# The rows of the second and later experts' tokens by an indirect transfer from DRAM instead of a one-hot matmul

## The reference

```python
def moe_swiglu(h, router_w, wg, wu, wd):
    logits = (h @ router_w).astype(jnp.float32)
    top_val, top_idx = lax.top_k(logits, TOP_K)
    w = jax.nn.softmax(top_val, axis=-1)
    gate = jnp.sum(jax.nn.one_hot(top_idx, N_EXPERTS, dtype=jnp.float32) * w[..., None], axis=-2).astype(h.dtype)
    out = jnp.zeros_like(h)
    for e in range(N_EXPERTS):
        out = out + gate[..., e:e + 1] * swiglu(h, wg[e], wu[e], wd[e])
    return out
```

## Time and profile before

| what | value |
|---|---|
| median of 3 runs | 1684.62 us |
| profiled execution: its own time | 1684.51 us |
| its span, first to last instruction | 1682.8 us |
| busy: PE, DVE, ACT, POOL | 1589.7, 1250.4, 1077.1, 23.4 us |
| mean granted TensorE clock | 0.961 of full speed |
| DRAM read and written | 432.49 MB, 1.05 MB |

### The profile page before, as it was taken

The page is one execution under the profiler, slowest core; times in us unless marked ns, Lnnn a source line. Parts: engine busy times, 40 slices in busy tenths (PEclk is TensorE's granted clock), DMA queues, the critical chain, the costliest instruction groups (busy, mean ns, idle before and its releaser), DMA issues.

```text
span 1682.8 us, 21706 instructions
## 1 busy us (share of the span) xinstructions
PE 1589.7 (94%) x7714; PEld 1317.2 (78%) x7715; DVE 1250.4 (74%) x1354; ACT 1077.1 (64%) x1276; POOL 23.4 (1%) x52
## 2 busy tenths in 40 slices
PE   6988789998999976999999999999999999999997
PEld 5767678886888766788888888888888888888885
DVE  4545345555524743898998998998998998998996
ACT  4454344444425451787877877877877877877874
POOL 5000000000000000000000000000000000000000
PEclk9999799999968996999999999999999999999999
DMA  9510244666421142799999999999999999999960
GB/s 359 202 46 0 76 150 158 217 226 237 166 101 51 35 141 100 255 388 357 357 359 344 370 360 346 363 364 339 376 359 337 376 353 343 371 361 342 365 247 25
DMA packets 199808, 434.15 MB, mean 258 GB/s; under 512 B 6906, under 2 KB 35668, under 8 KB 199764
## 3 DMA queue, kind: packets, MB, share of 16 engines
q1 hardware_dynamic: 197184, 432.22, 71.1%
q0 software_dynamic: 288, 1.05, 0.2%
q10 hardware_dynamic: 2292, 0.28, 0.1%
HBM read 432.49 MB, written 1.05 MB: 258 GB/s over the span
## 4 chain that ended last, share of the span: by engine, by line
PE 91%; DVE 4%; ACT 3%; issue 1%; ACTq 1%; DVEq 0%
PE ps L1145 18%; PE ps L1150 18%; PE ps L1147 18%; PE ps L637 8%; PE ps L640 7%; PE ps L643 7%; PE ps L768 3%; PE ps L1116 2%; PE ps L1171 1%; PE ps L709 1%; PE ps L733 1%; DVE f_w_lo L1631 1%; PE ps L951 1%; ACT f_w_hi L1249 1%; DVE hT_lo L1643 1%
## 5 line engine op out<-in xcount | busy, mean ns | idle before, releaser
L2140 DVE TENSOR_TENSOR w_lo<-ring,w_hi 128x1024 fp32r<-128x1024 f32 x672 | 813.5, 1224 | 55.7 <-ACT w_hi L1556 15.7
L1556 ACT ACTIVATE w_hi<-ring 128x1024 fp32r<-128x1024 f32 x672 | 712.3, 1062 | 185.0 <-PE ps L1150 185.0
L1145 PE MATMUL ps<-w_hi,x_hi 128*128 128x512 f32 x896 | 354.0, 395 | 2.4 <-DVE x_lo L2146 2.4
L1147 PE MATMUL ps<-w_hi,x_lo 128*128 128x512 f32 x896 | 350.0, 391 | 0.0
L1631 DVE TENSOR_TENSOR f_w_lo<-ring,f_w_hi 128x1024 fp32r<-128x1024 f32 (+1 forms) x139 | 169.0, 1225 | 145.3 <-ACT f_w_hi L1249 144.9
L1150 PE MATMUL ps<-w_lo,x_hi 128*128 128x512 f32 x896 | 276.6, 390 | 0.0
L1249 ACT ACTIVATE f_w_hi<-ring 128x1024 fp32r<-128x1024 f32 (+1 forms) x139 | 145.1, 1056 | 163.6 <-PE ps L643 155.1
L637 PE MATMUL ps<-f_w_hi,hT_hi 128*128 128x512 f32 (+2 forms) x480 | 187.2, 394 | 19.9 <-DVE hT_lo L1643 10.3
L1145 PEld LDWEIGHTS ps<-w_hi,x_hi 128*128 128x128 f32 x896 | 168.7, 188 | 36.8 <-issue 2.6
L1150 PEld LDWEIGHTS ps<-w_lo,x_hi 128*128 128x128 f32 x896 | 168.5, 188 | 36.3
L1147 PEld LDWEIGHTS ps<-w_hi,x_lo 128*128 128x128 f32 x896 | 168.8, 188 | 34.1
(11 more groups left out here) (250 smaller groups left out, 1284.9 us busy)
## 6 DMA issues: line engine op xcount, KB each, us to landing
ring<-in_moe_w_gate SPq DMA_DIRECT2D x56, 2048.0 KB, 8.5
ring<-in_moe_w_up SPq DMA_DIRECT2D x56, 2048.0 KB, 9.1
ring<-in_moe_w_down SPq DMA_DIRECT2D x56, 2048.0 KB, 8.2
ring<-in_ffn_w_gate SPq DMA_DIRECT2D x11, 1024.0 KB, 5.4
ring<-in_ffn_w_up SPq DMA_DIRECT2D x11, 1024.0 KB, 8.0
ring<-in_ffn_w_down SPq DMA_DIRECT2D x11, 1024.0 KB, 5.4
ring<-in_w_in_ab SPq DMA_DIRECT2D x5, 2048.0 KB, 17.6
ring<-in_w_in_c SPq DMA_DIRECT2D x5, 2048.0 KB, 12.7
```

The source lines that it names most:

```text
L1145: pe.matmul(ps[:, bnk, :], hi, w_h, start=first_ and (bnk != part.open), stop=False, skip_group_check=True)
L1147: pe.matmul(ps[:, bnk, :], lo, w_h, start=False, stop=False, skip_group_check=True)
L1556: sc_.activation(w_hi[:, high_e.k % STAGES, :], raw(slot, q), ACT.Copy).then_inc(hi_ready, 1)
L2140: ve.tensor_tensor(w_lo[:, st, :], raw(slot, q), w_hi[:, st, :].bitcast(F32), ALU.subtract).then_inc(lo_ready, 1)
```

## The change

Ahead of the experts POOL writes the normed tokens `h` to a DRAM tensor `token_rows`. At the end of an expert's step 5, PE multiplies `sel` with a column of token numbers (`find_rows`, 2 float32 matmuls with one column), DVE copies the 128 numbers to `row_of` as integers in step 6, and POOL starts an indirect transfer that brings these 128 rows of 4 KB from DRAM into `rows_in` (the first half of `h`, which the experts no longer read). In place of `gather` in the last step, PE waits for that transfer and transposes the rows (`turn_rows`, 8 transposes). The `gather` ahead of the first expert stays.

```diff
+        token = sb("token", [P, TT])
+        row_of = sb("row_of", [P, 1], U32)
...
+        rows_in = h[:, 0, :]
+        token_rows = nc.dram_tensor("token_rows", (S, D), F32).ap()
...
+            step(pool.iota(token[:, :], [[P, TT]], base=0, channel_multiplier=1, allow_small_or_imprecise_dtypes=True))
+
             pool.wait_ge(counts_ready, 1)
...
             pool.dma_start(fin_g, final_g.partition_broadcast(P)).then_inc(gains_loaded, 16)
+
+            t = Tally()
+
+            def fetch():
+
+                pool.wait_ge(row_of_ready, t.next(row_of_ready))
+                pool.sem_inc(rows_asked, 1)
+                pool.indirect_dma_start(rows_in, None, token_rows[:, :], bass.IndirectOffsetOnAxis(ap=row_of[:, 0:1], axis=0)).then_inc(rows_landed, 16)
+
+            pool.wait_ge(h_ready, 1)
+            pool.dma_start(token_rows.rearrange("(t p) d -> p t d", p=P), h[:, :, :]).then_inc(rows_stored, 16)
+            pool.wait_ge(rows_stored, 16)
+            pool.wait_ge(routed, 1)
+            n_more = pool.value_load(rounds[0:1, 0:1], min_val=NE - 1, max_val=2 * NE - 1)
+            fetch()
+            with t.loop(pool, 0, n_more, {row_of_ready: 1}) as it:
+                fetch()
...
+            def find_rows():
+
+                pe.wait_ge(sel_ready, t.next(sel_ready))
+                for tt in range(TT):
+                    mm = pe.matmul(ps[:, 7, S:S + 1], sel[:, tt, :], token[:, tt:tt + 1], start=(tt == 0), stop=(tt == TT - 1))
+                mm.then_inc(row_of_full, 1)
+
+            def turn_rows():
+
+                pe.wait_ge(rows_landed, t.next(rows_landed, 16))
+                for k in range(KD):
+                    mm = pe.transpose(ps[:, 2 + k // 4, (k % 4) * P:(k % 4 + 1) * P], rows_in[:, k * P:(k + 1) * P], ident[:, :])
+                mm.then_inc(gathered, 1)
+                t.next(gathered)
+
...
                     if s == LAST:
-                        gather()
+                        turn_rows()
...
                     if s == 4:
                         turn_sel()
+                    if s == LAST - 1:
+                        find_rows()
...
+                    if s == LAST:
+                        ve.wait_ge(row_of_full, t.next(row_of_full))
+                        ve.tensor_copy(row_of[:, :], ps[:, 7, S:S + 1]).then_inc(row_of_ready, 1)
                     low_e(slots["u", s])
```

More of the change, by code:

```diff
@@ L314, in build @@
         selT_full, selT_ready = sem("selT_full"), sem("selT_ready")
+        rows_stored, row_of_full, row_of_ready, rows_landed = (sem("rows_stored"), sem("row_of_full"), sem("row_of_ready"),
+                                                               sem("rows_landed"))
+        rows_asked = sem("rows_asked")
         scattered, added = sem("scattered"), sem("added")
@@ L1210, in _ @@
             with t.loop(pe, 0, n_more, {lo_ready: NPARTS, part_used: NPARTS, e_act_ready: ESTEPS, e_turned: ESTEPS,
-                                      sel_ready: 1, gathered: 1, scattered: 2, added: 2, selT_full: 1,
+                                      sel_ready: 1, rows_landed: 16, gathered: 1, scattered: 2, added: 2, selT_full: 1,
                                       out_hi_ready: 1, out_lo_ready: 1}) as it:
@@ L2189, in _ @@
             with t.loop(ve, 0, n_more, {hi_ready: NPARTS, e_silu_ready: ESTEPS, a_hi_ready: ESTEPS, x_hi_ready: 1,
-                                      scattered: 2, selT_full: 1, out_hi_ready: 1}) as it:
+                                      scattered: 2, selT_full: 1, row_of_full: 1, out_hi_ready: 1}) as it:
                 expert(LOOP_SLOTS, False, it + 1)
```

## The result

| | median | runs | profiled: own time, span |
|---|---|---|---|
| before | 1684.64 us | 4 (1684.47 to 1685.3) | 1684.51, 1682.8 us |
| after | 1655.22 us | 4 (1653.93 to 1656.63) | 1654.7, 1653.0 us |

The ratio is 0.9825 with a 95% interval of 0.9808 to 0.9842: 29.4 us faster, where 17.4 were forecast and 21.5 was the most that the range allowed. The question is where 12 us more came from.

What follows compares the result with a forecast made beforehand. PE's queue was taken to bound the experts. Per expert 3.58 - 0.87 - 0.44 = 2.27 us, less 0.1 wait, times 8 gives 17.4 us: 1684.5 to 1667.1 us, range 1663 to 1681.5.

Steps and rivals of the forecast that it cites:

- the total: Whole kernel: 8 x (2.27 - 0.1) = 17.4 us saved from 1684.5, giving 1667.1 us.
- Gather minus transposes: PE, each expert's last step: gather removed, 3.58 us, against eight transposes added, 0.87 us.
- `find_rows`: PE, end of step 5: two float32 matmuls, four records, add at most 0.44 us per expert.
- Period: Time between the experts' ends: 121.1 us instead of 123.37.
- The wait: PE ahead of the transposes: waits 0 to 0.34 us for the fetched rows per expert, taken as 0.1.
- the landing from issue: Row fetch: 8.1 us from issue to landing, after POOL's 512 KB load; up to 8.86 with index work.
- POOL's instruction: POOL's instruction for the indirect fetch was to take under 1 us.
- ACT's wait for `x_hi`: Experts' last step: ACT's wait for the gather, 2.5 us, was to be gone.
- Rival A: Index reading waits out a DVE w_lo: rows 0.8 to 1.6 us late, 8.6 us saved, 1676; chance 0.27.
- Rival B: Fetch over 10.8 us: PE's idle time exceeds 2.27 us, clock may fall, slower, 1698; 0.12 with rest of C.
- Rival C: Experts' weight stream becomes the bound: below 362 GB/s the period is 123.8 us, time 1688; 3 in 100.
- The estimate of 3.2 us for the fetch: From the skill, 2.0 us plus bytes at 436 GB/s: rows 5 us early, full 18.2 us saved; not used.

Runs made afterwards that it cites:

- e15_look_b: The kernel before, unchanged, one run: 1670.87 us, first expert at 666.60.
- e14_look_a: The kernel before, unchanged, one run: 1686.62 us, first expert at 680.71.
- e17_look_d: The changed kernel with its two tiles placed last and the iota behind the router, one run: 1669.77 us, first expert at 679.03.
- e13_pad64: The kernel before with one unused tile of 64 bytes a partition: 1670.62 us, ratio 0.9954.
- e6_after_again: The changed kernel, unchanged, measured again: 1652.74 us (1648.68 to 1658.26, 6 runs).
- e1: The kernel before plus the iota at 9 us and the two small tiles, nothing else: 1670.57 us, ratio 0.9945.
- e9: The kernel before with the change's two small tiles and nothing that uses them: 1670.23 us, ratio 0.9964.
- e12: The changed kernel with its two tiles placed last, so no other moves, and the iota behind the router: 1659.47 us, two groups, ratio 0.9887.
- e16: The changed kernel with its two tiles placed last and the iota behind the router, one run: 1654.81 us, first expert at 664.60.
- e7_early: The changed kernel with find_rows before step 5's e_down and the copy to row_of behind step 5's e_act, fetch 5.4 us sooner: 1655.12 us.
- e8_late: The changed kernel with the copy to row_of behind the four parts of u, 5.8 us later: 1718.02 us, ratio 1.0263.
- e10_iota_alone: The kernel before with the iota written into an existing tile, so no tile moves: 1685.05 us, ratio 1.0035.
- e4: The changed kernel with the iota after the other constants, at about 43 us: 1653.92 us.
- e5: The kernel before, unchanged: 4 runs at 1668.08 to 1671.56 us and 8 at 1684.51 to 1686.41.
- e2: The changed kernel with the gather kept, the fetch into its own tile and PE waiting for it behind the gather: 1669.07 us, ratio 0.9966.
- e3: The kernel before with eight transposes of h's first half instead of the gather, no rows looked up, stored or fetched: 1657.1 us, ratio 0.9894.
- e11: The kernel before with 8 extra 256-column matmuls of zeros among the 60-column ones from 485 us on: 1675.13 us, ratio 1.0001.

## Why the prediction was wrong in size and right in its steps

**The step that failed** is the total: "The profiled execution's own time is 1684.51 (span 1682.8 and 1.7 around it) ... so 1684.5 - 17.4 = 1667.1 us." It takes the 678.5 us ahead of the experts as fixed, and with them "some 0.2%" as all that a measurement can shift. All runs of before that I had stood within 0.8 us of each other, and all were of the long group. What the runs showed in place of this step: that stretch alone varies by 14 us from run to run of one program (680.71 and 666.60 us to the first expert), and the change's two small tiles, which I costed at nothing without a word, took the long case away. Compared like with like, spans:

| us | first expert | experts and end | span |
|---|---|---|---|
| short: before (e15_look_b) | 666.60 | 1002.6 | 1669.2 |
| short: after | 667.71 | 985.3 | 1653.0 |
| long: before (e14_look_a) | 680.71 | 1004.2 | 1684.9 |
| long: changed, tiles unmoved (e17_look_d) | 679.03 | 989.0 | 1668.0 |
| tiles moved: before (e13_pad64) | 671.59 | 1001.5 | 1673.1 |
| tiles moved: changed (e6_after_again) | 671.75 | 984.8 | 1656.5 |

The experts and the end gained 17.3 us in the short pair and 15.2 in the long one (e17_look_d had longer waits for rows, 1.1 us, and a slower end). The last pair is the cleanest: moved tiles and 10.2 us of low clock from 479.5 us on in both, so that the first expert starts within 0.2 us, and 16.8 us gained behind it. 29.8 = 17.3 + 1.7 that the long run lost in before's experts and end + 10.8 ahead of the experts. Even of the 17.3, 8 x 0.13 = 1.1 us belong to the moved tiles. In medians, with tiles moved on both sides, before has 1670.5 us (34 runs of e1, e9 and e13) and the changed kernel 1654.3 (10 runs of after and e6): 16.2 us, 1.0%, is what the change itself is worth, near the 17.4 forecast. The rest of the 29.4 us goes with the moved tiles (1684.6 to 1670.5), which keep the long case away.

**The terms.** Gather minus transposes: 2.71 forecast, 2.78 found. `find_rows`: 0.44 and 0.44. Period: 121.1 forecast, 121.13 found in after, with 0.13 of it saved by the moved tiles; with tiles unmoved it is 121.11, 121.30 and 121.68 in three profiles (e12, e17, e16), as the wait differs. **The wait:** 0.1 taken, 0.15 to 0.17 measured against e7_early, but with landings of 7.7 to 9.1 us it is 0.5 per expert in e16_look_c (3.4 / 7). That it came so near was partly luck, as two things were off and cancelled: the landing from issue is as the row said (7.9 against 8.1), but POOL's instruction starts 0.8 to 0.9 us after the copy has ended, which I had not counted, so that the rows come 8.4 to 9.3 us after the release in the seven experts of after (8.7 in the middle). PE, for its part, arrived 8.8 us after it (776.09 against 767.29), not 8.52. **POOL's instruction** was forecast under 1 us and took 1.63 to 1.69. It costs nothing beyond its part in the landing. ACT's wait for `x_hi` went from 17.6 to 0.6 us, as forecast.

**Rival A** did not come in its size: late by 0.6 at most in after and by 1.1 once in e16_look_c, whose mean of 0.5 is under A's 0.8 to 1.6 per expert. Yet the rows speak for its mechanism. POOL's instruction and the DVE instruction that runs when it starts, at the second fetch of after, e8_late and e7_early:

```profile
889.82 1.67 POOL L599 DMA_INDIRECT h<-token_rows,row_of  x1 [119.96 <-DVE row_of L2223]
889.42 1.23 DVE L2183 TENSOR_TENSOR w_lo<-ring,w_hi 128x1024 fp32r<-128x1024 f32 x1 [0.38 <-ACT w_hi L1599]
...
908.37 1.42 POOL L599 DMA_INDIRECT h<-token_rows,row_of  x1 [127.75 <-DVE row_of L2224]
907.72 5.23 DVE L2183 TENSOR_TENSOR w_lo<-ring,w_hi 128x1024 fp32r<-128x1024 f32 x4
...
888.28 1.24 POOL L599 DMA_INDIRECT h<-token_rows,row_of  x1 [119.64 <-DVE row_of L2229]
887.45 1.23 DVE L2183 TENSOR_TENSOR w_lo<-ring,w_hi 128x1024 fp32r<-128x1024 f32 x1
```

DVE's `w_lo` (the first of the four in e8_late's row) has 0.82, 0.58 and 0.40 us left, and POOL's instruction ends 0.84 us after it in each. So it is in all 72 indirect transfers of the nine profiles that have them: a `w_lo` runs when the instruction starts, and it ends 0.81 to 0.92 us after that `w_lo`, whatever was left of it (0.36 to 0.83 us). The Trainium skill (SBUF — State Buffer, "Who interferes with whom") makes a DVE instruction with two inputs in SBUF contend with a GpSimd one that reads SBUF, and the rows agree with that: they are what one would see if POOL's instruction waited for the end of the one that DVE runs. Still, three placements are three points, no run has DVE idle there, and what in the instruction waits is not shown. If it is so, it costs 0.8 us in after where the rival took 1.22, and the landing of 7.9 us from the issue has it in it. **Rival B** is a real mechanism at another distance (e8_late). **Rival C** did not come: DMA's share rose to 1.00 with 369 GB/s, and no engine waits for the ring. The estimate of 3.2 us for the fetch by the Trainium skill (DMA: Bandwidth & Descriptors, the anatomy of one SWDGE DMA) is too low here: 5.1 us for the last one, which has no weight stream beside it, 7.9 with it.

**What stays open:** why the places of tiles decide whether the long case can occur, and which tile it is. The only direct trace is in the last section. What makes the low clock long in one run and short in the next goes with where it falls (the table there), but what sets that place is open too.

## What to carry to other kernels

A few runs that agree within 0.1% do not show that a kernel has one time: look in the profile for a stretch where TensorE's clock is low for tens of microseconds while it is busy, ask what the total would be if it were short, and put that in the range. Compare two kernels by stages, at points that the change does not touch, before the whole difference is put down to the change. For a fetch that is to be in time, count from the release and not from the issue; its trigger 5 us sooner gave 0.15 us per expert, and 6 us later cost 8.

## What was not expected of the hardware

- In each of the 19 profiles the granted clock fell at 474.7 to 481.7 us, behind matmuls of 48 columns, and came back after 3.4, 6.8, 10.2 or 30.7 us. With tiles unmoved, 3.4, 10.2 and 30.7 were seen; 30.7 in each profile of a long run (three of before, e10_iota_alone, e17_look_d), in no other. How long it stays low goes with where in the program it falls, counted from the start of the first 48-column matmul of that block, and the classes do not overlap:

| from the first 48-column matmul to the fall | low for | profiles |
|---|---|---|
| 2.64 to 2.75 us | 10.2 us | after, e4, e6, e7, e8, e12, e13 |
| 2.87 to 3.13 us | 30.7 us | before, e5, e10, e14, e17 |
| 3.70 us | 6.8 us | e9 |
| 5.30 to 6.00 us | 3.4 us | e1, e2, e3, e11, e15, e16 |

A tenth of a microsecond parts 10.2 from 30.7 us. So it fits the 19 profiles that moved tiles shift the fall out of the third of a microsecond that makes a run long; what sets the place of the fall no run shows.

- The dense SwiGLU's matmuls with `hT_hi` (L637, 240 to 405 us) follow each other at a mean of 238.1 to 238.2 ns from start to start (144 to 146 records) in every kernel whose tiles stand as before (before, e3, e5, e10, e11, e12, e14 to e17), and at 235.9 to 236.2 ns in every one with moved tiles (after, e1, e2, e4, e6 to e9, e13). That is 0.3 us in all, and 0.13 us in each expert's period, but it shows that PE's pace can go with where the kernel's tiles lie.
- An indirect transfer of 128 rows of 4 KB keeps POOL for 1.2 to 1.7 us, until 0.81 to 0.92 us after the end of the two-input DVE instruction that runs when it starts. It starts 0.8 to 0.9 us after the DVE copy that it waits for, and lands 7.3 to 9.9 us after its issue beside the weight stream (63 transfers), 4.2 to 5.1 us without it (9).
